# Scores of two key groups in one block-diagonal product; three steps of the second half put in another order

## The chip, the cores and the metric

The kernel runs on one NeuronCore of one Trainium2 chip. The metric is the device time of one execution in microseconds (us), and a kernel's time is the median of its runs.

## The reference

The kernel computes two transformer blocks on 512 tokens of width 1024, all in float32. The first block is a feed-forward layer, a mixing layer, a second feed-forward layer; the second block is a retention layer and a stick-breaking attention layer. The change touches only the attention of the mixing layer, which has three groups of four heads of width 64:

```
DILATED_GROUPS = ((128, 1), (512, 4), (2048, 16))      # window, dilation of each group
q, k, v = parts of (u @ w_in), each (1, 512, 12 heads, 64)
q, k = apply_partial_rope(q), apply_partial_rope(k)    # rotates the first 16 of 64 columns
for each group g:  s = q . k * 64 ** -0.5 over the keys that the window allows
                   m = max(s);  p = exp(s - m);  o = p @ v / sum(p)
alpha = softmax over the three groups of their log denominators;  o = sum(alpha * o)
```

## The kernel before

Every float32 product is made of three passes on TensorE (PE): an operand is split into a rounded high part (written by ScalarE, ACT) and the rest (written by VectorE, DVE: source minus high part), and `passes` multiplies high by high, high by low and low by high. Weights come in slabs through SyncE's queue into two slots `raw`; ACT writes `w_hi` (L668), DVE writes `w_lo` (L1377), and only then may PE use the slab (`w_ready`). All engines run their own program in order, joined by semaphores. The order of the work is written out by hand in each engine's block.

**Halves.** The mixing attention runs twice, a = 0 and a = 1, each for two of the four heads of every group. In a half, `qk` makes q and k of the three groups (g = 0, 1, 2; o = 0 for q, 1 for k): PE projects (512 columns, 24 passes), ACT copies the high part to `stage` (L689), DVE the low part (L1401), PE multiplies with a rotation matrix (`rotate`, L2614, L2615), DVE forms the two rope products (L1716, L1725) and their sum (L1728), and `rope_done` splits the result. In `rope_done` the three groups are treated unlike:

- g = 0: rows 0 to 63 of the tile are one head, rows 64 to 127 the other. ACT writes `q_both` or `k_both` in two instructions of 64 rows each (L908), and DVE writes `q_low` or `k_rest` in two of 64 rows (L1739). Then GpSimd's queue moves half tiles to the other 64 rows.
- g = 1, 2, k: one ACT instruction of 128 rows writes `k_hi[:, g - 1]` (L900) and one DVE instruction writes `k_lo[:, g - 1]` (L1731).
- g = 1, 2, q: ACT writes `q_pair[:, 0]` (L905), DVE writes `q_pair[:, 1]` in two instructions of 256 columns (L1734), and GpSimd's queue copies it (L618) into `q_head[j]`, which holds head j's 64 rows and zeros in the other 64.

After `qk` DVE and ACT do the pooling branch (half 0 alone: `pool_row`, L1827; `pool_window`, L1837 to L1842; `pool_low`) and the split of the values (`mix_values`: ACT L934, DVE L1453, reading two blocks of `values` at a time). DVE's program is one list: `rope_done` of the last k, the four pool rows, and among these the `w_lo` of the slabs that PE's `values` need.

**Units.** A half has 8 attention units (4 residues of the token number times 2 heads). `scores(a, k)` makes 768 scores a row: a mask over 512 keys of group 0 (L2675), a mask over 256 keys of groups 1 and 2 (L2676), group 0's product in two passes of 512 columns (L2677, L2678), and for each of groups 1 and 2 three passes of 128 columns (L2449, L2450, L2451 with `q_head`). DVE takes the row maximum (L1773), ACT the exponential (L941), PE turns it with six transposes (`turn`, L2692) into two banks of `acc`, ACT and DVE split it (L961 and L963, L1796 and L1798), PE multiplies with the values (L2717), and DVE adds the two parts (L1812), which gives the two banks back (`acc_free`). `attend` issues on PE, for each k: `scores(k + 3)`, `turn(k + 1)`, `values of k`, and for k of 4 and over some filling passes. `scores(a, k)` for k of 2 and over waits until the exponential of unit k - 2 is taken.

In half 1 PE runs the four blocks of the last `values` with the other steps between: the last rotation after block 0, `first_score(1)` after block 1, `scores(1, 1)` after block 2, then `attend`. DVE takes both maxima and then splits the last values; ACT likewise takes both exponentials and then the last values.

Of the kernel before, what the change touches and what calls it, by code (L numbers as in the profile page):

```python
# [17 lines left out]
F32 = mybir.dt.float32  # L18
# [5 lines left out]
P = 128  # L24
# [86 lines left out]
def block_kernel(nc, dram, out):  # L111
    with ExitStack() as ctx:
# [8 lines left out]
        with ExitStack() as under:  # L121
            q_both = [sb(f"q_both{j}", [P, TOK], F32R, under) for j in range(2)]
            k_both = [sb(f"k_both{j}", [P, TOK], F32R, under) for j in range(2)]
            k_rest = [sb(f"k_rest{j}", [P, TOK], F32R, under) for j in range(2)]
            q_pair = sb("q_pair", [P, 2, TOK], F32R, under)
# [116 lines left out]
        with ExitStack() as scope:  # L242
# [13 lines left out]
            with ExitStack() as inner:  # L256
                q_head = [sb(f"q_head{j}", [P, 2, N_GROUPS - 1, TOK], F32R, inner) for j in range(2)]
                k_hi = sb("k_hi", [P, N_GROUPS - 1, TOK], F32R, inner)
                k_lo = sb("k_lo", [P, N_GROUPS - 1, TOK], F32R, inner)
                va = sb("va", [P, TB, N_GROUPS * GROUP_HEADS, 2, HEAD], F32R, inner)  # L260
                stage = sb("stage", [P, 4 * KEYS], F32R, inner)
                fold = sb("fold", [P, 3 * HEAD], F32, inner)
                rope_a = sb("rope_a", [P, 2, TOK], F32, inner)
                band = sb("band", [P, 2 * DIL - 1, P], mybir.dt.bfloat16, inner)
                classes = sb("classes", [P, 2, P], mybir.dt.bfloat16, inner)
                ident_b = sb("ident_b", [P, P], mybir.dt.bfloat16, inner)
                neg_max = sb("neg_max", [P, UNITS], F32, inner)
                den = sb("den", [P, UNITS], F32, inner)
                rden = sb("rden", [P, UNITS], F32, inner)
                rcount = sb("rcount", [P, 2 * PAD], F32, inner)  # L270
                mix_b11 = sb("mix_b11", [P, TB, TOK // 2], F32, inner)
                mix_b12 = sb("mix_b12", [P, TB, TOK // 2], F32, inner)
                mix_b22 = sb("mix_b22", [P, TB, TOK // 2], F32, inner)
# [140 lines left out]
        pair_low_ready = sem("pair_low_ready")  # L414
        head_landed = sem("head_landed")
# [156 lines left out]
        def _(pool):  # L572
# [29 lines left out]
            for j, rows in enumerate(head_rows[::-1]):  # L602
                nc.gpsimd.memset(k_rest[j][rows, :].bitcast(F32), 0.0).then_inc(rest_clear, 1)
                nc.gpsimd.memset(q_head[j][rows, :, :, :].bitcast(F32), 0.0).then_inc(rest_clear, 1)

            def other_halves(a):
# [8 lines left out]
                for g in range(N_GROUPS - 1):  # L615
                    pool.wait_ge(pair_low_ready, (N_GROUPS - 1) * a + g + 1)
                    for j in range(2):
                        pool.dma_start(q_head[j][own[j], :, g, :], q_pair[own[j], :, :]).then_inc(head_landed, 16)  # L618
# [37 lines left out]
        def _(act):  # L656
            n, s, u, b = Count(), Count(), Count(), Count()
            val, turn, pairs = Count(), Count(), Count()
# [235 lines left out]
            def rope_done(g, o):  # L894
# [4 lines left out]
                if g and o:  # L899
                    ins = nc.scalar.activation(k_hi[:, g - 1, :], t(o), ACT.Copy, scale=QK_SCALE[o])  # L900
                elif g:
                    if pairs.k:
                        act.wait_ge(head_landed, 2 * 16 * pairs.k)
                    pairs.next()
                    ins = nc.scalar.activation(q_pair[:, 0, :], t(o), ACT.Copy, scale=QK_SCALE[o])  # L905
# [111 lines left out]
            exps(0)  # L1017
            exps(1)
            mix_values(2, 1)
# [347 lines left out]
        def _(dve):  # L1367
# [354 lines left out]
            def rope_done(g, o, split_after):  # L1722
# [7 lines left out]
                if g and o:  # L1730
                    stt(k_lo[:, g - 1, :], t(o), QK_SCALE[o], k_hi[:, g - 1, :].bitcast(F32), ALU.mult, ALU.subtract).then_inc(op_ready, 1)  # L1731
                elif g:
                    for j, cols in enumerate((EARLY, LATE)):
                        stt(q_pair[:, 1, cols], t(o)[:, cols], QK_SCALE[o], q_pair[:, 0, cols].bitcast(F32),  # L1734
                            ALU.mult, ALU.subtract).then_inc(pair_low_ready if j else op_ready, 1)
                    dve.wait_ge(pair_low_ready, lows.next())
# [159 lines left out]
            scores(0)  # L1896
            scores(1)
            mix_values(2, 1)
# [525 lines left out]
        def _(pe):  # L2424
# [242 lines left out]
            def scores(a, k):  # L2667
# [11 lines left out]
                for g in range(N_GROUPS - 1):  # L2679
                    last = passes(narrow[:, P * g:P * (g + 1)], [q_head[head][:, i, g, plain[r]] for i in range(2)],  # L2680
                                  (k_hi[:, g, plain[r]], k_lo[:, g, plain[r]]), False, g == N_GROUPS - 2)
# [58 lines left out]
            def first_score(a):  # L2740
                pe.wait_ge(op_ready, op.at())
                pe.wait_ge(rest_clear, 4)
                pe.wait_ge(both_landed, 4 * 16 * (a + 1))
                pe.wait_ge(head_landed, 2 * (N_GROUPS - 1) * 16 * (a + 1))
# [14 lines left out]
            def first_query(c):  # L2759
# [5 lines left out]
                if c == DC - 1:  # L2765
# [5 lines left out]
            values(x, plain, {(0, DC - 1): lambda: rotate_last(1), (1, DC - 1): lambda: first_score(1),  # L2771
                              (2, DC - 1): lambda: scores(1, 1)})
# [396 lines left out]
def lay_out(a):  # L3169

    w = {}
    for f, full in zip(("ffn1", "ffn2"), FULL):
# [11 lines left out]
    w["mix_qk"] = np.stack([np.stack([np.stack([cols[2 * g + c], cols[qc + 2 * g + c]], 1)  # L3184
                                      for g in range(N_GROUPS)]) for c in range(2)]).reshape(2, N_GROUPS, P, SLAB)
# [100 lines left out]
```

## Time and profile before

| | us |
|---|---|
| median of 3 runs | 1863.39 (1862.91 to 1864.31) |
| the profiled execution, its own time | 1862.57 |
| its span | 1860.8 |
| PE busy in the span | 1845.2 (99%) |
| PE weight loads busy | 1627.8 (87%) |
| DVE busy | 1324.6 (71%) |
| ACT busy | 879.1 (47%) |
| mean granted TensorE clock | 0.998 |

The span is the time from the first to the last instruction of the program; some 1.8 us of the execution lie around it. A matmul is shown with a duration that contains the latency of the array, so PE looks busy where one matmul's tail covers a short wait: what a pass costs is the distance from its start to the next start, and what a wait costs is what that distance has too much.

### The profile page before, as it was taken

How to read it: one execution, taken by the hardware profiler on the slowest of the kernel's cores; microseconds unless marked ns; L12 is line 12 of the kernel's file. 1: busy time of each engine (PE TensorE's matmuls, PEld its weight loads, DVE VectorE, ACT ScalarE, POOL GpSimd, SP SyncE). 2: the span in 40 equal slices, each digit the busy share in tenths (PEclk: the TensorE clock that was granted, in tenths of full speed). 3: DMA queues.
4: the chain of work that ended last, by engine and by line, in shares of the span. 5: the costliest groups of instructions: out<-in, count | busy, mean ns of one | idle time of the engine just before them, and what ended most of it. 6: DMA issues, size and time to landing. Idle time of an engine off the chain costs nothing.

```text
span 1860.8 us, 27165 instructions
## 1 busy us (share of the span) xinstructions
PE 1845.2 (99%) x10801; PEld 1627.8 (87%) x10807; DVE 1324.6 (71%) x1778; ACT 879.1 (47%) x1170; POOL 73.3 (4%) x96
## 2 busy tenths in 40 slices
PE   9999999999999999999999999999999999999997
PEld 7998998888889989989998888888888888888886
DVE  8875887888778888856888745463647776666666
ACT  6652664435355535634653332423336644444445
POOL 0000000120000000000000000000000000000000
PEclk9999999999999999999999999999999999999999
DMA  6744763462317526654753222122221222212213
GB/s 213 184 122 125 197 171 101 176 151 70 118 46 210 147 91 175 164 160 123 195 153 117 91 91 91 68 93 79 99 88 48 91 88 72 91 70 88 90 68 91
DMA packets 51506, 218.86 MB, mean 118 GB/s; under 512 B 5856, under 2 KB 8448, under 8 KB 39888
## 3 DMA queue, kind: packets, MB, share of 16 engines
q1 hardware_dynamic: 38960, 180.90, 28.9%
q0 software_dynamic: 12016, 36.04, 9.8%
q8 instruction: 69, 1.13, 0.2%
q10 hardware_dynamic: 432, 0.56, 0.1%
q14 instruction: 29, 0.24, 0.0%
HBM read 205.41 MB, written 5.77 MB: 113 GB/s over the span
## 4 chain that ended last, share of the span: by engine, by line
PE 73%; DVE 5%; ACT 2%; issue 1%; DMA 0%; DVEq 0%; POOL 0%; ACTq 0%
PE acc L2449 16%; PE acc L2451 16%; PE acc L2450 16%; PE acc L2456 4%; PE acc L2455 4%; PE acc L2457 4%; PE att L2450 2%; PE att L2451 2%; PE att L2449 2%; DVE w_lo L1377 1%; PE att L2455 1%; PE att L2457 1%; PE att L2456 1%; PE acc L2717 1%; PE acc L2692 1%
## 5 line engine op out<-in xcount | busy, mean ns | idle before, releaser
L1377 DVE TENSOR_TENSOR w_lo<-raw,w_hi 128x2048 fp32r<-128x2048 f32 (+1 forms) x120 | 271.0, 2258 | 69.8 <-ACT w_hi L668 68.9
L668 ACT ACTIVATE w_hi<-raw 128x2048 fp32r<-128x2048 f32 (+1 forms) x120 | 226.1, 1884 | 120.5 <-PE acc L2451 106.3
L2449 PE MATMUL acc<-x_hi,w_hi 128*128 128x512 f32 x712 | 280.9, 394 | 0.6 <-DVE x_lo L1440 0.3
L2451 PE MATMUL acc<-x_hi,w_lo 128*128 128x512 f32 x712 | 277.4, 390 | 0.0
L2450 PE MATMUL acc<-x_lo,w_hi 128*128 128x512 f32 x712 | 277.3, 389 | 0.0
L2449 PEld LDWEIGHTS acc<-x_hi,w_hi 128*128 128x128 f32 x712 | 133.7, 188 | 30.5 <-issue 2.9
L2450 PEld LDWEIGHTS acc<-x_lo,w_hi 128*128 128x128 f32 x712 | 133.7, 188 | 29.0 <-issue 1.6
L2451 PEld LDWEIGHTS acc<-x_hi,w_lo 128*128 128x128 f32 x712 | 133.7, 188 | 28.0
L2455 PE MATMUL acc<-xt_hi,w_hi 128*128 128x256 f32 x516 | 144.5, 280 | 0.0
L2457 PE MATMUL acc<-xt_hi,w_lo 128*128 128x256 f32 x516 | 144.3, 280 | 0.0
L2456 PE MATMUL acc<-xt_lo,w_hi 128*128 128x256 f32 x516 | 144.3, 280 | 0.0
L2450 PE MATMUL acc<-g_lo,w_hi 128*128 128x512 f32 x352 | 137.0, 389 | 0.0
L2449 PE MATMUL acc<-g_hi,w_hi 128*128 128x512 f32 x352 | 137.0, 389 | 0.0
L2451 PE MATMUL acc<-g_hi,w_lo 128*128 128x512 f32 x352 | 136.9, 389 | 0.0
L767 ACT ACTIVATE tmp<-acc 128x256 f32<-128x256 f32 x172 | 65.3, 380 | 80.2 <-PE acc L2457 72.8
L2455 PEld LDWEIGHTS acc<-xt_hi,w_hi 128*128 128x128 f32 x516 | 98.2, 190 | 0.0
L2456 PEld LDWEIGHTS acc<-xt_lo,w_hi 128*128 128x128 f32 x516 | 96.9, 188 | 0.0
L2457 PEld LDWEIGHTS acc<-xt_hi,w_lo 128*128 128x128 f32 x516 | 96.9, 188 | 0.0
L2455 PE MATMUL acc<-x_hi,wc_hi 128*128 128x256 f32 x344 | 95.0, 276 | 0.0
L2457 PE MATMUL acc<-x_hi,wc_lo 128*128 128x256 f32 x344 | 95.0, 276 | 0.0
L2456 PE MATMUL acc<-x_lo,wc_hi 128*128 128x256 f32 x344 | 94.9, 276 | 0.0
L2451 PEld LDWEIGHTS acc<-g_hi,w_lo 128*128 128x128 f32 x352 | 66.1, 188 | 13.7
(487 smaller groups left out, 4663.5 us busy)
## 6 DMA issues: line engine op xcount, KB each, us to landing
raw<-in_ret_head SPq DMA_DIRECT2D x24, 1024.0 KB, 4.8
raw<-in_ffn_down SPq DMA_DIRECT2D x32, 704.0 KB, 4.2
raw_c<-in_ffn_seven SPq DMA_DIRECT2D x37, 512.0 KB, 5.2
raw<-in_ffn_seven SPq DMA_DIRECT2D x33, 512.0 KB, 4.8
raw<-in_ffn_seven POOLq DMA_DIRECT2D x33, 512.0 KB, 7.6
raw<-in_ffn_seven SPq DMA_DIRECT2D x37, 256.0 KB, 4.6
raw<-in_ret_out SPq DMA_DIRECT2D x8, 1024.0 KB, 4.7
raw<-in_sb_v SPq DMA_DIRECT2D x8, 1024.0 KB, 4.7
```

The lines of the kernel that those rows point to most:

```text
L668: nc.scalar.activation(w_hi[:, slot, at:at + cols], raw[:, slot, 0:cols], ACT.Copy).then_inc(w_hi_ready, 1)
L767: nc.scalar.activation(dst, src, ACT.Copy).then_inc(snap_ready, 1)
L1377: tt(w_lo[:, slot, at:at + cols], raw[:, slot, 0:cols], w_hi[:, slot, at:at + cols].bitcast(F32), ALU.subtract).then_inc(w_ready, 1)
L2449: mm(dst, still[0], move[0], start=first, stop=False)
L2450: mm(dst, still[0], move[1], start=False, stop=False)
L2451: return mm(dst, still[1], move[0], start=False, stop=last)
L2455: mm(dst, still[0], move[0], start=first, stop=False, skip_group_check=True)
L2456: mm(dst, still[0], move[1], start=False, stop=False, skip_group_check=True)
L2457: return mm(dst, still[1], move[0], start=False, stop=last, skip_group_check=True)
L2692: last = nc.tensor.transpose(dst[i // TB][:, P * (i % TB):P * (i % TB) + P], tmp[:, at:at + P], ident[:])
L2717: last = mm(dst, va[:, k_blk, value_slot(g, head)].rearrange("p s d -> p (s d)"), turned_probs[:, k % 2, i].rearrange("p s q -> p (s q)"), ...
```

## The change

1. **Weights laid out by head.** In `mix_qk`, slabs 1 and 2 of a half no longer hold group 1 and group 2 with two heads each; slab 1 + j holds head j of both: rows 0 to 63 of a projected tile are group 1, rows 64 to 127 group 2.
2. **Block diagonals of k.** `k_hi` and `k_lo` become [128, 2 heads, 2, 512]: of head j, the first 512 columns have group 1's k in rows 0 to 63 and zeros below, the second 512 have zeros above and group 2's k in rows 64 to 127. ACT and DVE write them in two instructions of 64 rows each; the low part of the second counts on a new semaphore `half_low_ready`, and DVE waits for it before it goes on. GpSimd sets the zeros (four memsets of 64x1024 in the place of two of 64x2048).
3. **q without copies.** q of groups 1 and 2 is written straight to `q_hi` and `q_lo` by one instruction each; `q_pair`, `q_head`, their eight DMAs and ACT's wait for them go.
4. **Scores.** Three passes of 256 columns take the place of six of 128.
5. **Order of half 1.** `first_score(1)` comes after block 2 of the last values, `scores(1, 1)` after block 3; DVE and ACT split the last values between the first and the second maximum and exponential.

```diff
-                q_head = [sb(f"q_head{j}", [P, 2, N_GROUPS - 1, TOK], F32R, inner) for j in range(2)]
-                k_hi = sb("k_hi", [P, N_GROUPS - 1, TOK], F32R, inner)
-                k_lo = sb("k_lo", [P, N_GROUPS - 1, TOK], F32R, inner)
+                q_hi = sb("q_hi", [P, 2, TOK], F32R, inner)
+                q_lo = sb("q_lo", [P, 2, TOK], F32R, inner)
+                k_hi = sb("k_hi", [P, 2, 2, TOK], F32R, inner)
+                k_lo = sb("k_lo", [P, 2, 2, TOK], F32R, inner)
...
@@ GpSimd
-                nc.gpsimd.memset(q_head[j][rows, :, :, :].bitcast(F32), 0.0).then_inc(rest_clear, 1)
+                for part in (k_hi, k_lo):
+                    nc.gpsimd.memset(part[rows, :, j, :].bitcast(F32), 0.0).then_inc(rest_clear, 1)
...
-                for g in range(N_GROUPS - 1):
-                    pool.wait_ge(pair_low_ready, (N_GROUPS - 1) * a + g + 1)
-                    for j in range(2):
-                        pool.dma_start(q_head[j][own[j], :, g, :], q_pair[own[j], :, :]).then_inc(head_landed, 16)
@@ ACT, rope_done
                 if g and o:
-                    ins = nc.scalar.activation(k_hi[:, g - 1, :], t(o), ACT.Copy, scale=QK_SCALE[o])
+                    for i, rows in enumerate(head_rows):
+                        ins = nc.scalar.activation(k_hi[rows, g - 1, i, :], t(o)[rows, :], ACT.Copy, scale=QK_SCALE[o])
                 elif g:
-                    if pairs.k:
-                        act.wait_ge(head_landed, 2 * 16 * pairs.k)
-                    pairs.next()
-                    ins = nc.scalar.activation(q_pair[:, 0, :], t(o), ACT.Copy, scale=QK_SCALE[o])
+                    ins = nc.scalar.activation(q_hi[:, g - 1, :], t(o), ACT.Copy, scale=QK_SCALE[o])
@@ ACT, half 1
             exps(0)
+            mix_values(2, 1)
             exps(1)
-            mix_values(2, 1)
@@ DVE, rope_done
                 if g and o:
-                    stt(k_lo[:, g - 1, :], t(o), QK_SCALE[o], k_hi[:, g - 1, :].bitcast(F32), ALU.mult, ALU.subtract).then_inc(op_ready, 1)
+                    for i, rows in enumerate(head_rows):
+                        stt(k_lo[rows, g - 1, i, :], t(o)[rows, :], QK_SCALE[o], k_hi[rows, g - 1, i, :].bitcast(F32),
+                            ALU.mult, ALU.subtract).then_inc(half_low_ready if i else op_ready, 1)
+                    dve.wait_ge(half_low_ready, lows.next())
                 elif g:
-                    for j, cols in enumerate((EARLY, LATE)):
-                        stt(q_pair[:, 1, cols], t(o)[:, cols], QK_SCALE[o], q_pair[:, 0, cols].bitcast(F32),
-                            ALU.mult, ALU.subtract).then_inc(pair_low_ready if j else op_ready, 1)
-                    dve.wait_ge(pair_low_ready, lows.next())
+                    stt(q_lo[:, g - 1, :], t(o), QK_SCALE[o], q_hi[:, g - 1, :].bitcast(F32), ALU.mult, ALU.subtract).then_inc(op_ready, 1)
@@ DVE, half 1
             scores(0)
+            mix_values(2, 1)
             scores(1)
-            mix_values(2, 1)
@@ PE, scores
-                for g in range(N_GROUPS - 1):
-                    last = passes(narrow[:, P * g:P * (g + 1)], [q_head[head][:, i, g, plain[r]] for i in range(2)],
-                                  (k_hi[:, g, plain[r]], k_lo[:, g, plain[r]]), False, g == N_GROUPS - 2)
+                last = passes(narrow[:, 0:2 * P], (q_hi[:, head, plain[r]], q_lo[:, head, plain[r]]),
+                              (k_hi[:, head, :, plain[r]], k_lo[:, head, :, plain[r]]), False, True)
@@ PE, first_score
-                pe.wait_ge(rest_clear, 4)
+                pe.wait_ge(rest_clear, 6)
                 pe.wait_ge(both_landed, 4 * 16 * (a + 1))
-                pe.wait_ge(head_landed, 2 * (N_GROUPS - 1) * 16 * (a + 1))
+                pe.wait_ge(half_low_ready, (N_GROUPS - 1) * (a + 1))
@@ PE, half 1
-            values(x, plain, {(0, DC - 1): lambda: rotate_last(1), (1, DC - 1): lambda: first_score(1),
-                              (2, DC - 1): lambda: scores(1, 1)})
+            values(x, plain, {(0, DC - 1): lambda: rotate_last(1), (2, DC - 1): lambda: first_score(1),
+                              (3, DC - 1): lambda: scores(1, 1)})
@@ lay_out
+    def one_head(first, c, j):
+        return np.concatenate([cols[first + 2 * g + c][..., HEAD * j:HEAD * (j + 1)] for g in range(1, N_GROUPS)], -1)
+
+    w["mix_qk"] = np.stack([np.stack([np.stack([cols[c], cols[qc + c]], 1)]
+                                     + [np.stack([one_head(0, c, j), one_head(qc, c, j)], 1) for j in range(2)])
+                            for c in range(2)]).reshape(2, N_GROUPS, P, SLAB)
```

## Rows read from the trace of the kernel before

**Rows 1.** The page, busy time of each engine, us, share, instructions.
```profile
PE 1845.2 (99%) x10801; PEld 1627.8 (87%) x10807; DVE 1324.6 (71%) x1778; ACT 879.1 (47%) x1170; POOL 73.3 (4%) x96
```
**Rows 2.** Busy time of PE, PEld, DVE, ACT, POOL (instructions), clock, DMA, in one stretch.
```profile
386.00:428.00 42.00, 41.93 (x263) 37.23 (x263) 34.81 (x52) 16.10 (x19) 7.39 (x8) 1.00 0.60 146
```
**Rows 3.** Timeline of PE, start and duration in us: 256-column and 128-column passes, a turn.
```profile
498.73 0.28 PE L2451 MATMUL acc<-w_hi,x_lo 128*128 128x256 f32 x1
...
501.11 0.28 PE L2451 MATMUL acc<-w_hi,x_lo 128*128 128x256 f32 x1
...
511.33 0.22 PE L2449 MATMUL att<-k_hi,q_head 128*128 128x128 f32 x1
...
511.95 0.84 PE L2692 MATMUL acc<-ident,tmp 128*128 128x128 f32 x6
```
**Rows 4.** Timeline of PE, ACT and DVE through one attention unit, and the next turns.
```profile
519.78 0.85 PE L2692 MATMUL acc<-ident,tmp 128*128 128x128 f32 x6
...
520.44 0.60 ACT L961 ACTIVATE stage<-acc 128x512 fp32r<-128x512 f32 x1 [1.11 <-PE acc L2692]
...
521.14 0.69 DVE L1796 TENSOR_TENSOR stage<-acc,stage 128x512 fp32r<-128x512 f32 x1 [0.26 <-ACT stage L961]
...
522.08 0.41 DVE L1812 TENSOR_REDUCE o_even<-acc 128x128 f32<-128x256 f32 x1
...
522.64 0.84 PE L2692 MATMUL acc<-ident,tmp 128*128 128x128 f32 x6
...
528.37 0.30 PE L2692 MATMUL acc<-ident,tmp 128*128 128x128 f32 x1
```
**Rows 5.** Timeline of DVE, half 0: rope_done of k (g = 0), q and k (g = 1).
```profile
372.13 0.69 DVE L1728 TENSOR_TENSOR tmp<-tmp 128x512 f32<-128x512 f32 x1
374.16 1.41 DVE L1739 SCALAR_TENSOR_TENSOR k_rest<-tmp,k_both 64x512 fp32r<-64x512 f32 x2 [1.34 <-ACT k_both L908]
375.60 0.69 DVE L1401 TENSOR_TENSOR stage<-acc,stage 128x512 fp32r<-128x512 f32 x1
...
379.72 0.69 DVE L1728 TENSOR_TENSOR tmp<-tmp 128x512 f32<-128x512 f32 x1
...
381.90 0.69 DVE L1401 TENSOR_TENSOR stage<-acc,stage 128x512 fp32r<-128x512 f32 x1
...
383.83 0.69 DVE L1728 TENSOR_TENSOR tmp<-tmp 128x512 f32<-128x512 f32 x1
...
385.94 0.69 DVE L1401 TENSOR_TENSOR stage<-acc,stage 128x512 fp32r<-128x512 f32 x1
```
**Rows 6.** Timeline of DVE and PE weight loads, half 0, where its first values begin.
```profile
405.31 2.29 DVE L1377 TENSOR_TENSOR w_lo<-raw,w_hi 128x2048 fp32r<-128x2048 f32 x1
...
407.65 0.19 PEld L2449 LDWEIGHTS acc<-w_hi,x_hi 128*128 128x128 f32 x1 [0.43 <-DVE w_lo L1377]
```
**Rows 7.** Timeline of DVE and PE, entry of half 0 into its units.
```profile
437.42 0.88 DVE L1453 SCALAR_TENSOR_TENSOR va<-acc,r_tok,va 128x256 fp32r<-128x256 f32 x2 [1.86 <-ACT va L934]
...
442.80 0.85 PE L2692 MATMUL acc<-ident,tmp 128*128 128x128 f32 x6 [0.18 <-DVE o_even L1812]
```
**Rows 8.** Timeline of PE, DVE and ACT, entry of half 1 into its units.
```profile
497.92 0.51 PE L2614 MATMUL att<-stage,rot_r 128*128 128x512 f32 x1 [0.53 <-DVE stage L1401]
...
500.81 0.69 DVE L1731 SCALAR_TENSOR_TENSOR k_lo<-tmp,k_hi 128x512 fp32r<-128x512 f32 x1 [0.70 <-ACT k_hi L900]
...
502.17 0.27 PE L2676 MATMUL att<-classes,ident_b 128*128 128x256 bf16 x1 [0.79 <-DMA q_head<-q_pair]
...
508.18 1.81 DVE L1773 TENSOR_REDUCE neg_max<-att 128x1 f32<-128x768 f32 x2
509.15 0.90 ACT L941 ACTIVATE tmp<-att,neg_max 128x768 f32<-128x768 f32 x1 [6.27 <-DVE neg_max L1773]
...
511.80 0.88 DVE L1453 SCALAR_TENSOR_TENSOR va<-acc,r_tok,va 128x256 fp32r<-128x256 f32 x2 [1.81 <-ACT va L934]
...
512.63 0.38 PE L2675 MATMUL att<-band,ident_b 128*128 128x512 bf16 x1
```

More of the change, by code:

```diff
@@ L124, in block_kernel @@
             k_rest = [sb(f"k_rest{j}", [P, TOK], F32R, under) for j in range(2)]
-            q_pair = sb("q_pair", [P, 2, TOK], F32R, under)
         h = sb("h", [P, DC, TOK])
@@ L413, in block_kernel @@
         both_landed = sem("both_landed")
-        pair_low_ready = sem("pair_low_ready")
-        head_landed = sem("head_landed")
+        half_low_ready = sem("half_low_ready")
         park_landed = sem("park_landed")
@@ L657, in _ @@
             n, s, u, b = Count(), Count(), Count(), Count()
-            val, turn, pairs = Count(), Count(), Count()
+            val, turn = Count(), Count()
             def prep(cols=SLAB, seg=0):
@@ L3183, in lay_out @@
     qc = heads // P
-    w["mix_qk"] = np.stack([np.stack([np.stack([cols[2 * g + c], cols[qc + 2 * g + c]], 1)
-                                      for g in range(N_GROUPS)]) for c in range(2)]).reshape(2, N_GROUPS, P, SLAB)
+    def one_head(first, c, j):
[3 more added lines that the diff above has]
+                            for c in range(2)]).reshape(2, N_GROUPS, P, SLAB)
     v_cols = columns(w_in, 2 * heads, heads).reshape(P, DC, N_GROUPS, 2, 2 * HEAD)
```

## The prediction

> **What bounds the kernel now.** I read the page's busy times first: PE is busy 99% of the span [rows 1], so a saving on PE seems to be worth its full length. That figure hides short waits, so I then read starts. In the stretch where half 0 goes from rope to pooling PE shows 41.93 of 42 us busy, but DVE has 34.81 [rows 2], and what remains to DVE is waits for ACT within its own chain. The first matmul of that half's first values starts only when DVE has finished `w_lo`: 405.31 + 2.29 = 407.60, start at 407.65 [rows 6]. So there DVE sets PE's time, with no slack.
>
> The timeline of the units gives the second bound. Turns on PE start at 519.78 and 522.64, 2.86 apart with a unit's scores between; the two steps from there to 528.37, one with scores and one with filling passes in their place, take 5.73 = 2 x 2.865 [rows 4]. The same period for unlike work says that the loop is not PE's own. It closes as: turn at 519.78, ACT splits at 520.44 (+0.66), DVE at 521.14 (+0.70), DVE's reduction at 522.08 (+0.94) ends at 522.49 (+0.41) and gives the banks back, and the next turn starts 0.15 later at 522.64. 0.66 + 0.70 + 0.94 + 0.41 + 0.15 = 2.86. The turn at 442.80 in half 0 even shows its wait for that reduction [rows 7]. PE is a co-bound: free of waits a turn starts about 0.1 after the last pass of the scores, so its own loop would be some 0.05 shorter at best. It is not longer than the chain.
>
> **The change part by part.** All against the profiled execution, 1862.57.
>
> *Scores.* Six passes of 128 columns took from 511.33 to 511.95 = 0.62. A 256-column pass costs (501.11 - 498.73) / 21 = 0.113 [rows 3], three of them 0.34. Saved on PE: 0.28 a unit, 16 units, 4.5 us. The loads of the q tiles are halved with them. The strided second level of the new moving tile is not in the trace; its bounds are 0 (as the two-level tiles of the values) and the whole saving, if each row of 128 went at the old price. I take 0.
>
> How much of it reaches the end? In a half, units 3 to 7 are scored inside the 2.86 loop. What PE saves there it waits: 0. In half 0, units 0 to 2 are scored before the loop. But DVE comes to its split of the values at 437.42 after waiting for ACT [rows 7], ACT was at the exponential of unit 1, that waited for the maximum of unit 1, and this stood behind DVE's pooling; from 437.42 DVE's list runs without a gap to the first split of the turned unit. That chain contains no pass of scores. So half 0 gives 0 of its 2.2 us, bound 0 to 0.3 (a little where PE waits in the pooling). Half 1 is worked out below.
>
> *q.* One instruction in the place of two of 256 columns and a wait. With two, sum to next step is 379.72 to 381.90 = 2.18; with one instruction of 512 columns, as k now, 383.83 to 385.94 = 2.11 [rows 5]. -0.07 for each q that lies on DVE's chain. The eight copies leave GpSimd's queue; what stood behind them there (copies for `mix_b`) comes some 6 us earlier and is needed a hundred us later in half 1. 0.
>
> *k.* This is the price. Two ACT and two DVE instructions of 64 rows take the place of one and one of 128 rows. Group 0 already does so, and its rows show that 64 rows cost as long as 128: DVE's two take 1.41 together, against 0.69 for one of 128, and it waits 1.34 for ACT where the wait for one is 0.70. From the sum to the next step: 372.13 to 375.60 = 3.47 for the split k, 2.11 for the whole one [rows 5]. +1.36 us for each k of groups 1 and 2, four of them, all on DVE's chain. Bounds: 0.6, if the second halves would run beside other work, to 1.5.
>
> *Half 0.* Behind the first such k stand on DVE: the low part of the next projection, its rope, and through ACT's order the next `w_hi`; behind the second one the four pool rows and the `w_lo` of rows 6. I find no idle time there that isn't a wait for ACT that itself waited for DVE. So 1.36 + 1.36 - 0.07 = 2.65 goes to the `w_lo` that PE waits for at 407.65, and from there PE, DVE and ACT shift together. Half 0: +2.65 (bounds +1.0 to +3.0).
>
> *Half 1.* Times in the frame of before. The first k and the two q move DVE by 1.36 - 2 x 0.07, and by 0.11 more because the step after this k didn't wait for its end and now does: +1.33. The low part that the last rotation waits for comes that much later, so PE's rotation at 497.92 [rows 8] goes to 499.25. Block 1 begins 0.58 after it (its third pass was at 498.73, less two of 0.113), and blocks 1 and 2 with 24 passes each end at 499.83 + 2 x 2.72 = 505.3. The low part of the second k ended at 500.81 + 0.69 = 501.5 and ends 1.33 + 1.36 later, at 504.2, so `first_score` in its new place doesn't wait, and the wait for the q copies (0.79 shown) is gone. Up to here PE is only some 1 us late and saves 0.28 twice more. But DVE: the next `w_lo` waits for `w_hi`, and this for ACT's second half of k: 1.33 + 0.64 (1.34 - 0.70 of rows 5) + 0.1, since the two halves don't overlap in ACT as whole ones did, is 2.1 later than before; the sums for `mix_b` follow and the first maximum starts at 508.18 + 2.1 = 510.28.
> Now the new order. Exponential 0 starts 0.97 after the maximum (508.18 to 509.15), at 511.25; ACT then splits the last values from 512.15 (0.90); DVE follows 0.87 later, at 513.02 (before, 511.80 stood about that far behind ACT's start, two exponentials after 509.15), takes 0.79, and only then the maximum of unit 1: 513.81. Its exponential runs 514.80 to 515.79. `scores(1, 3)` on PE waits for exactly this one; it starts at 515.86, before at 512.63 [rows 8]: 3.23 later, less the 0.28 saved in it, and the turn of unit 1 and with it the loop of 2.86 come 2.95 later. Before, the exponential of unit 1 followed that of unit 0 at once (0.90 behind 509.15), was over by 511, and nobody waited for it. So half 1 costs +2.9, of which 2.1 come from k and 0.8 from the order; the seven savings of scores in it do nothing. Bounds: -0.6, if PE's list set the entry (next part), to +3.5.
>
> *Memsets.* The same bytes in four pieces; they are over some 50 us before they are needed. 0.
>
> Sum: 2.65 + 2.9 = +5.55; 1862.57 + 5.55 = 1868.1. The median shown is 0.82 above the profiled execution, so I say 1868.9.
>
> **The rivals.**
> (1) *PE is the bound after all.* For it: 99% busy, and the waits that go, 0.79 at the first score. Then the 4.5 of the passes and 0.8 of the wait come through and DVE's added time lies beside PE: 1863.39 - 5.3 = 1858.1. Against it: the period of 2.86 with and without scores, and rows 6. I give it 0.10. Here the trace can be weighed against the Trainium skill ("TensorE: Matmul & The Clock Gate", Back-to-back issue gap): by it an isolated pass costs the columns / 2.4 plus 2.5 ns, so 56 ns for 128 columns, and six narrow passes would cost no more than three wide ones; this rival would then give back only the 0.8 of the wait, 1862.6. Rows 3 disagree: 0.62 / 6 = 0.10 us for a narrow pass, nearly that of a wide one. Whoever leaves this out loses nothing of the sum.
> (2) *PE's list sets the entry of half 1.* Half 0 costs 2.65, but DVE and ACT in half 1 have enough room; then half 1 has the rotation +1.33, the wait -0.95 (0.79 shown, with what the tail covers), and three scores -0.84: -0.5. 1863.39 + 2.15 = 1865.5. For it: DVE sat idle 1.81 before 511.80, room in which a delay could vanish. Against it: that room is a wait for ACT behind exponential 1, and the new order puts one more such wait in. 0.20.
> (3) *The split runs beside itself*, so that each k costs about 0.7: half 0 +1.3, half 1 +2.2, 1866.9. Against it: the 1.41 and 1.34 of rows 5. 0.08.
> The forecast: 0.62.
>
> **How the numbers follow.** Faster or slower by over 0.2% (3.7 us) is about what a measurement of this kernel tells from no change. Forecast, 1868.9 +-1.5, lies at +5.5; nearly all of it is slower. (2) and (3) are within 0.2%, with some of each beyond. (1) is faster. Faster 0.11, same 0.27, slower 0.62. The range leaves out (1) and takes in (2): 1863.5 to 1870.7.
>
> **What would show it.** In the profile after: the k splits of 64 rows on DVE twice 0.69; the first matmul of half 0's values still waiting for `w_lo`, 2.6 later (at 410.2 to 410.4); turns in the units still 2.86 apart, now with a wait of about 0.3 for the reduction in front of each; in half 1 a wait of PE for an exponential of several us in front of the third and fourth scores. I would be wrong if the period fell to about 2.6, if the first values of half 0 began before 409, or if the fourth scores of half 1 found their exponential taken.

## The result and the profile after

The kernel after takes 1868.88 us (median of 11 runs, 1867.58 to 1870.71), the kernel before, beside it, 1862.90 (11 runs, 1862.43 to 1864.31): ratio 1.0031, 95% interval 1.0023 to 1.0039. It is 6.0 us slower; 1868.9 had been forecast, which is 5.5 above the 1863.39 of before that the forecast started from. The profiled execution of after took 1869.26 us, its span is 1867.4.

The page's busy times answer to [rows 1]. PE is busy 2.7 us less and the kernel is 6 us longer:

```profile
PE 1842.5 (99%) x10753; PEld 1623.2 (87%) x10759; DVE 1327.2 (71%) x1778; ACT 881.4 (47%) x1174; POOL 68.6 (4%) x90
```

The stretch of [rows 2], same columns. PE had 41.93 busy there and has 39.36:

```profile
386.00:428.00 42.00, 39.36 (x242) 34.74 (x242) 34.94 (x52) 14.44 (x17) 5.99 (x6) 1.00 0.53 132
```

Those 2.57 us are one wait. The first line is DVE's and the second PE's timeline at the first values of half 0, as in [rows 6]:

```profile
408.28 2.28 DVE L1371 TENSOR_TENSOR w_lo<-raw,w_hi 128x2048 fp32r<-128x2048 f32 x1
...
410.62 0.39 PE L2443 MATMUL acc<-w_hi,x_hi 128*128 128x256 f32 x1 [2.57 <-DVE w_lo L1371]
```

Why DVE's list came later is in its timeline of one k, which answers to the last part of [rows 5]. From the sum to the next step it takes 387.62 - 384.15 = 3.47 (2.11 before):

```profile
384.15 0.69 DVE L1722 TENSOR_TENSOR tmp<-tmp 128x512 f32<-128x512 f32 x1
386.19 1.40 DVE L1726 SCALAR_TENSOR_TENSOR k_lo<-tmp,k_hi 64x512 fp32r<-64x512 f32 x2 [1.34 <-ACT k_hi L897]
387.62 0.69 DVE L1395 TENSOR_TENSOR stage<-acc,stage 128x512 fp32r<-128x512 f32 x1
```

The entry of half 1, PE, DVE and ACT together, answers to [rows 8]:

```profile
502.25 0.50 PE L2608 MATMUL att<-stage,rot_r 128*128 128x512 f32 x1 [1.94 <-DVE stage L1395]
...
513.34 0.95 DVE L1767 TENSOR_REDUCE neg_max<-att 128x1 f32<-128x768 f32 x1
514.33 0.90 ACT L935 ACTIVATE tmp<-att,neg_max 128x768 f32<-128x768 f32 x1 [6.35 <-DVE neg_max L1767]
...
515.37 0.39 PE L2669 MATMUL att<-band,ident_b 128*128 128x512 bf16 x1 [1.69 <-ACT tmp L935]
...
516.08 0.88 DVE L1447 SCALAR_TENSOR_TENSOR va<-acc,r_tok,va 128x256 fp32r<-128x256 f32 x2 [1.79 <-ACT va L928]
...
516.87 1.81 DVE L1767 TENSOR_REDUCE neg_max<-att 128x1 f32<-128x768 f32 x2
517.85 0.90 ACT L935 ACTIVATE tmp<-att,neg_max 128x768 f32<-128x768 f32 x1 [1.81 <-DVE neg_max L1767]
...
519.13 0.27 PE L2670 MATMUL att<-classes,ident_b 128*128 128x256 bf16 x1 [1.79 <-ACT tmp L935]
```

PE waits for each of the first two exponentials (515.37, 519.13), and the second stands behind the last values: split (516.08), maximum (516.87), exponential (517.85). The loop answers to [rows 4]; PE's turns stay 2.86 apart, the last of them again with a wait shown for DVE's reduction:

```profile
522.46 0.28 PE L2445 MATMUL att<-k_hi,q_lo 128*128 128x256 f32 x1
522.89 0.85 PE L2685 MATMUL acc<-ident,tmp 128*128 128x128 f32 x6
...
525.75 0.85 PE L2685 MATMUL acc<-ident,tmp 128*128 128x128 f32 x6
...
531.48 0.73 PE L2685 MATMUL acc<-ident,tmp 128*128 128x128 f32 x5 [0.15 <-DVE o_odd L1806]
```

By starts, the turn comes 522.89 - 522.46 = 0.43 behind the last pass of the scores. A pass costs 0.12, so PE waits about 0.31 there. In before the last pass of the scores stands in front of the turn at 522.64 [rows 4] like this:

```profile
522.48 0.27 PE L2451 MATMUL att<-k_hi,q_head 128*128 128x128 f32 x1
```

That is 0.16, with 0.11 for a pass, so a wait of 0.05. What the scores save has turned into a wait.

To compare kernels I measure starts from the first rotation of half 0 (360.71 in before, 361.11 in after; what PE runs ahead of it is the same). The turn of the last unit starts at 96.41 in before and 98.95 in after for half 0, and at 170.52 and 176.10 for half 1: +2.54, and 3.04 more. What follows differs by under 0.7.

### The profile page after: what moved, and what is told of

The parts are those of the page before. It is cut to its first block, busy times and chain, and to the rows that moved or that the text cites. A ratio compares the mean times of both kernels' runs of the same rounds, so it can differ in the third digit from the quotient of the medians.

```text
span 1867.4 us, 27066 instructions
## 1 busy us (share of the span) xinstructions
PE 1842.5 (99%) x10753; PEld 1623.2 (87%) x10759; DVE 1327.2 (71%) x1778; ACT 881.4 (47%) x1174; POOL 68.6 (4%) x90
## 3 DMA queue, kind: packets, MB, share of 16 engines
q8 instruction: 68, 1.11, 0.2%
## 4 chain that ended last, share of the span: by engine, by line
PE 71%; DVE 6%; ACT 2%; issue 1%; DVEq 0%; ACTq 0%
PE acc L2443 16%; PE acc L2445 16%; PE acc L2444 16%; PE acc L2449 4%; PE acc L2450 4%; PE acc L2451 4%; PE att L2444 2%; PE att L2445 2%; PE att L2443 2%; DVE w_lo L1371 1%; PE att L2449 1%; PE att L2451 1%; PE att L2450 1%; DVE tmp L1722 0%; DVE tmp L1719 0%
## 5 line engine op out<-in xcount | busy, mean ns | idle before, releaser
L2443 PE MATMUL acc<-w_hi,x_hi 128*128 128x512 f32 (+1 forms) x224 | 77.0, 344 | 2.6 <-DVE w_lo L1371 2.6
```

Of the source, the lines that this page charges most:

```text
L2443: mm(dst, still[0], move[0], start=first, stop=False)
```

## The experiments

Each kernel was timed beside the kernel before. Its medians in the three groups of runs were 1862.85, 1862.97 and 1862.92. A start that stands in no line below, like 49.65, is measured from the first rotation of half 0.

**The order alone.** After with half 1's order as it was in before:

```
-  exps(0); mix_values(2, 1); exps(1)                      # ACT
+  exps(0); exps(1); mix_values(2, 1)
-  scores(0); mix_values(2, 1); scores(1)                  # DVE
+  scores(0); scores(1); mix_values(2, 1)
-  (2, DC - 1): first_score(1), (3, DC - 1): scores(1, 1)  # PE
+  (1, DC - 1): first_score(1), (2, DC - 1): scores(1, 1)
```

> The changed kernel with its block diagonals, but PE, DVE and ACT of half 1 in the order of before: first scores after block 1 of the last values, second after block 2, last values split behind both maxima. Theory (the exponential of unit 1 sets the entry of half 1, and the new order puts a split of the values in front of it): PE waits about 1.8 us for the low part of k in front of the first scores, but the exponential of unit 1 then runs right behind that of unit 0, the wait in front of the fourth scores (1.9 us in the changed kernel) is gone, and the turns of units 2 and on come 0.8 us earlier: 1868.0 against 1868.9. Rival (the new order is needed to hide the late k): the 1.8 us wait of PE is carried to the end, 1870 or more.

1867.65 us, ratio 1.0025 (1.0016 to 1.0035): 1.2 less than after. PE's timeline, the first scores and the turn of unit 2:

```profile
507.38 0.38 PE L2669 MATMUL att<-band,ident_b 128*128 128x512 bf16 x1 [1.63 <-DVE k_lo L1726]
...
521.85 0.85 PE L2685 MATMUL acc<-ident,tmp 128*128 128x128 f32 x6
```

The first scores now wait 1.63 for `k_lo`, but both exponentials follow one another and the fourth scores find theirs taken; the turn of unit 2 comes 0.96 earlier (521.85 - 361.03 against 522.89 - 361.11). The new order costs about 1 us, as worked out (0.8), and not more. The other 5 are not its doing.

**The split alone.** Before, with k of groups 1 and 2 split in two instructions of 64 rows on ACT and on DVE, into the same tiles. DVE and PE's first scores wait for the second half, as in after:

```
-  nc.scalar.activation(k_hi[:, g - 1, :], t(o), ...)
+  for rows in head_rows:
+      nc.scalar.activation(k_hi[rows, g - 1, :], t(o)[rows, :], ...)      # and k_lo alike
```

> The kernel before with one thing of the change: ACT and DVE write k_hi and k_lo of groups 1 and 2 in two instructions of 64 rows each, into the same tiles; q, its copies, scores and order as before. Theory (the split k lies on the DVE chain that PE waits for): the first matmul of half 0's first values comes 2.7 us later (407.65 to 410.3), half 1 enters its units 2.1 us later, sum +4.8: 1867.7 against 1862.9. Rival (PE is the bound and DVE's work lies beside it): 1862.9.

1869.00 us, ratio 1.0032 (1.0022 to 1.0043). No pass of PE is changed and the whole loss is there: rival (1) is out. It is 1.3 above what was expected. The first values come at 49.65 (46.94 in before): +2.71, as expected. But the last turn of half 0 comes 3.86 late, and half 1 adds 2.53 where 2.1 had been expected. What half 0 has too much in this execution is in the clock. These are windows around that wait; the seventh figure of a row, behind the length and the five engines, is the granted clock as a share of 2.4 GHz. Under them stands PE's timeline:

```profile
408.00:412.00 4.00, 1.66 (x8) 1.66 (x9) 3.89 (x5) 2.93 (x2) 1.93 (x2) 0.72 1.19 176
412.00:416.00 4.00, 4.00 (x32) 4.00 (x32) 3.70 (x7) 0.07 (x1) 0.00 (x0) 0.85 1.16 186
```

```profile
410.34 0.58 PE L2454 MATMUL acc<-w_hi,x_hi 128*128 128x256 f32 x1 [2.73 <-DVE w_lo L1379]
410.72 0.41 PE L2455 MATMUL acc<-w_lo,x_hi 128*128 128x256 f32 x1
...
413.06 0.34 PE L2454 MATMUL acc<-w_hi,x_hi 128*128 128x256 f32 x1
413.24 0.28 PE L2455 MATMUL acc<-w_lo,x_hi 128*128 128x256 f32 x1
...
413.70 0.28 PE L2456 MATMUL acc<-w_hi,x_lo 128*128 128x256 f32 x1
```

From 410.72 to 413.06 a pass takes 2.34 / 11 = 0.213, then (413.70 - 413.24) / 4 = 0.115. So after its wait PE ran at its lower level of 1.2 GHz; twelve passes cost 12 x 0.098 = 1.2 us. The profile of after shows a clock of 1.00 behind the same wait. How many of the eight runs had such a fall is not on record; three list a mean clock of 0.997, the others 0.998, so the median's 1.3 is not fully explained.

**Six narrow passes.** After, with 3 x 128 columns for each of groups 1 and 2 in place of 3 x 256:

```
-  last = passes(narrow[:, 0:2 * P], (q_hi[:, head, plain[r]], q_lo[:, head, plain[r]]),
-                (k_hi[:, head, :, plain[r]], k_lo[:, head, :, plain[r]]), False, True)
+  for g in range(N_GROUPS - 1):
+      last = passes(narrow[:, P * g:P * (g + 1)], (q_hi[:, head, plain[r]], q_lo[:, head, plain[r]]),
+                    (k_hi[:, head, g, plain[r]], k_lo[:, head, g, plain[r]]), False, g == N_GROUPS - 2)
```

> The changed kernel with the scores of groups 1 and 2 in six passes of 128 columns instead of three of 256, from the same block diagonals. Theory (what scores save on PE is waited away): 0.28 us a unit come back on PE, 4.5 us in all, but the turns stay 2.86 us apart, with the wait in front of them gone, and the total moves by +0.3 us (one pass group behind the awaited exponential in half 1), at most +0.6: 1869.2. Rival (PE is the bound): +4.5, 1873.4.

1869.08 us, ratio 1.0034 (1.0021 to 1.0047), after 1868.88: no difference that six runs can show. PE's timeline in half 1:

```profile
522.72 0.85 PE L2686 MATMUL acc<-ident,tmp 128*128 128x128 f32 x6
...
525.59 0.84 PE L2686 MATMUL acc<-ident,tmp 128*128 128x128 f32 x6
```

The turns stay 2.87 apart, and the last one comes 0.28 later than in after, as expected of one group of passes behind an awaited exponential. The wide passes, the point of the new layout, are worth next to nothing in this kernel, and not 4.5 us.

**The reduction first.** After, with DVE's reduction of a finished unit ahead of the low parts of the next:

```
-  if k + 1 < UNITS: low_probs(k + 1)
   dve.wait_ge(mixed, mix.next())
   nc.vector.tensor_reduce(o_unit[k % 2][:, k // 2, :], ...).then_inc(acc_free, 2)
+  if k + 1 < UNITS: low_probs(k + 1)
```

> The changed kernel with one step of DVE in the units moved: the reduction that gives back the two banks (L1806) now stands before the split of the next turned unit (L1790, L1792), not behind it. Theory (the loop of 2.86 us is turn, ACT split, DVE split, DVE reduction, next turn): the reduction leaves the loop, and where DVE has no weights to split (half 1, up to the fifth turn) the period falls to PE's own 2.53 to 2.6 us, about 0.3 less for 4 steps; in half 0 DVE's work of some 2.8 us a unit takes over, -0.1 us a unit. Sum -1.3 us: 1867.6. Rival (the period has another cause, PE or the exponentials): no change, 1868.9.

1867.77 us, ratio 1.0029 (1.0019 to 1.0038). The timeline of this kernel's PE in half 1:

```profile
525.19 0.82 PE L2685 MATMUL acc<-ident,tmp 128*128 128x128 f32 x6
...
527.72 0.82 PE L2685 MATMUL acc<-ident,tmp 128*128 128x128 f32 x6
```

The turns are 2.53 apart: the chain over DVE's reduction was what held the loop at 2.86. From the second turn to the last half 1 takes 15.61, 1.5 less than after (17.15). The whole kernel gains 1.1, near the 1.3 expected. The low parts of the last unit now come late and take something back: its values wait 0.82 in each half (a line of this wait stands below, in the kernel with all edits). This profiled execution also had two falls of the clock (0.81 in 408 to 412, 0.58 in 502 to 506); what the median has of them is not shown.

**The low part earlier.** After, with one step of DVE's list moved:

```
-  pool_window(i)
   if i == 1: prep()          # w_lo of the first values
+  pool_window(i)
```

> The kernel after, with one step of VectorE's list moved: in the first half the low part of the weights of the first values (w_lo, 2.28 us, it started at 408.28 and ended PE's wait of 2.57 us at 410.62) is formed before the pooling window of the second row instead of behind it. Theory: what lies between the end of the split of k and the loop is VectorE's whole list, so the first values start about 2.4 us earlier, but the later instructions of the list (pooled rows, maxima, low part of the turned probabilities) come no earlier, and the turn of unit 2 of half 0 stays at 84.6 us behind the first rotation: total 1868.9 (1867.5 to 1869.5). If it is the wait of PE at that place which costs the time: 1866.5. If only the fall of the granted clock behind that wait costs something now and then, the median is about 1868 and the spread of the runs is narrower.

1869.76 us, ratio 1.0039 (1.0025 to 1.0052), against 1868.9 expected: no gain, as the theory has it. It is 0.9 above after, which five runs do not set clear of noise (1868.40 to 1870.58, after 1867.58 to 1870.71), but the trace shows a loss that the theory had not. The first values come 2.7 earlier (46.82), and PE waits 13 us later. First DVE's, then PE's timeline:

```profile
411.51 1.12 DVE L1395 TENSOR_TENSOR pool_lo<-tmp,pool_hi 128x512 fp32r<-128x512 f32 x1 [1.19 <-ACT pool_hi L681]
```

```profile
423.71 0.39 PE L2443 MATMUL acc<-w_hi,x_hi 128*128 128x256 f32 x1 [3.43 <-DVE w_lo L1371]
```

In after the `w_lo` filled the time in which DVE waits for `pool_hi` of row 1; moved, it leaves 1.19 idle there, and DVE's next steps come 1.07 later. Behind the wait of 3.43 the clock fell too (seventh figure):

```profile
424.00:428.00 4.00, 4.00 (x24) 4.00 (x23) 3.79 (x9) 0.38 (x1) 0.00 (x0) 0.60 0.75 260
```

The slow passes of the values make DVE wait 2.17 for ACT's part of them, in after 1.40; that is the other 0.77 of the 1.83 by which the turn of unit 2 comes later. Four of the five runs list a mean clock of 0.997 or less and take 1869.6 to 1870.6; the fifth lists 0.998 and takes 1868.40. So the edit's own loss may be smaller than the medians say. What counts is DVE's whole list with its idle times, and not where in it PE's wait shows. The next edits follow from that.

**Fill the gap.** After, with a `w_lo` formed while ACT writes the `k_hi` of the last group (half 0: the one that stood in front; half 1: the one that stood behind, for which ACT also writes its `w_hi` before its part of `rope_done`):

```
   tt(t(o), t(o), t(2 + o), ALU.add)          # the sum, in rope_done
+  prep()                                     # w_lo
   dve.wait_ge(hi_ready, hi.next())
```

> The kernel after, with VectorE's forming of a low part of weights (2.28 us in half 0, 1.76 us in half 1) put into the 1.34 us in which VectorE waits for ScalarE's two half instructions k_hi of the last key group, in both halves; ScalarE's high part of the same slab comes before its part of the split in half 1. Theory (the split costs because VectorE's list is the bound and stands idle 1.34 us beside it): half 0 gains 1.3 (the idle time) and up to 2.3 at the first values, half 1 gains 1.3: total 1866.3 (1865 to 1867.5). Rival, that the split's own 0.7 us of VectorE per instruction and the chain k_hi, k_lo, DMA of the second half of k set the time: nothing gained or 1 us lost, 1869 to 1870, since k_lo comes 0.9 us later.

1864.54 us, ratio 1.0011 (1.0002 to 1.0020): 4.3 less than after, more than expected (2.6). DVE's timeline in half 0, sum, `w_lo`, `k_lo`, without idle time:

```profile
392.18 0.69 DVE L1722 TENSOR_TENSOR tmp<-tmp 128x512 f32<-128x512 f32 x1
392.79 2.28 DVE L1371 TENSOR_TENSOR w_lo<-raw,w_hi 128x2048 fp32r<-128x2048 f32 x1
394.99 1.40 DVE L1728 SCALAR_TENSOR_TENSOR k_lo<-tmp,k_hi 64x512 fp32r<-64x512 f32 x2
```

The turn of unit 2 of half 0 goes from 84.62 to 82.22: 2.4 = the 1.34 at `k_hi`, and 1.11 that this `w_lo` itself had waited for `w_hi` in its old place. The latter I had not counted. The last turn comes 3.98 earlier.

**The same on before.** Before with that edit:

> The kernel before, with the edit of f1_fill_the_gap alone (low part of the weights formed in the time in which VectorE waits for k_hi). Theory: in before PE is the bound at the entry of half 0 (its turn of unit 2 in g came only 0.2 us earlier), and half 1 gains the 0.7 us of the gap at most: 1862.4 (1861.8 to 1863.2). So what f1 gave back, 4.3 us, was the cost of the split; with the gap filled in both, the split still costs f1 - g1 = about 2 us. Rival, that f1's edit is worth as much without the split: 1858.6.

1863.07 us, ratio 1.0001 (0.9992 to 1.0010). It gains nothing, so what it gave after was the price of the split. The 0.7 expected in half 1 doesn't come either: the `w_lo` takes 1.75 in a gap of 0.70, `k_lo` comes that much later, and PE's first scores wait for it:

```profile
502.93 0.27 PE L2676 MATMUL att<-classes,ident_b 128*128 128x256 bf16 x1 [1.18 <-DVE k_lo L1733]
```

With the gap filled in both, the change costs 1864.54 - 1863.07 = 1.5.

**Halves that overlap.** After, with a semaphore for the first of ACT's two halves, so that DVE's first half runs beside ACT's second:

```
+  if i == 0: ins.then_inc(half_high_ready, 1)                 # ACT, behind each k_hi
-  dve.wait_ge(hi_ready, hi.next())                            # DVE
+  if g and o: dve.wait_ge(half_high_ready, highs.next())
+  else: dve.wait_ge(hi_ready, hi.next())
   ...
   for i, rows in enumerate(head_rows):
+      if i: dve.wait_ge(hi_ready, hi.next())
       stt(k_lo[rows, g - 1, i, :], ...)
```

> The kernel after, with a semaphore of its own for the first of ScalarE's two half instructions k_hi, so that VectorE forms the first half of k_lo while ScalarE forms the second half of k_hi: VectorE's idle time at a split of k goes from 1.34 to 0.67 us. Theory (VectorE's list is the bound, three of the four splits of k lie in it): 0.67 less at each, 2.0 us in all, 1866.8 (1866 to 1867.8). Rival, that only the number of instructions costs and the wait is hidden: 1868.9.

1866.69 us, ratio 1.0021 (1.0012 to 1.0030): 2.2 less than after, 2.1 forecast. DVE's timeline, idle time 0.70 in place of 1.34:

```profile
385.16 1.40 DVE L1734 SCALAR_TENSOR_TENSOR k_lo<-tmp,k_hi 64x512 fp32r<-64x512 f32 x2 [0.70 <-ACT k_hi L898]
```

Three splits at 0.64 are 1.9, the last turn comes 1.85 earlier: 1.26 in half 0, 0.59 in half 1.

**All together, with the change and without it.** On top of the filled gap: the three sums of `mix_b` (3.7 us of DVE) go from the entry of half 1 into the second `qk`, the reduction goes first, and PE and ACT enter half 1 in another order (DVE's stays that of after, and is put so in the kernel without the change too):

```
   elif last and g == 0: gather(0)                                      # DVE, in qk
+      <the three sums of mix_b>
-  {(0, ..): rotate_last(1), (2, ..): first_score(1), (3, ..): scores(1, 1)}
+  {(1, ..): rotate_last(1), (3, ..): (first_score(1), scores(1, 1))}
-  mix_values(2, 0); exps(0); mix_values(2, 1); exps(1)                  # ACT
+  mix_values(2, 0); mix_values(2, 1); exps(0); exps(1)
```

> f1 and three more edits on the kernel after: the three sums of mix_b (3.7 us of VectorE) go from the entry of half 1 to the first step of the second pass over q and k; PE runs the last rotation behind the second block of values and the first two scores behind the fourth; VectorE reduces a finished unit ahead of the next unit's low parts (the edit of e4_reduce_first), and ScalarE and VectorE take the last values ahead of the first exponentials. Theory (VectorE's list bounds the entries of both halves and its place in the loop costs 0.3 us a unit): half 0 -2.3 - 1.3, half 1 -1.5 - 3.7 (of which the second pass over q and k gives back up to 3.7, its idle time there is 0.2 to 1.3 us a step) - 1.5: 1859.5 (1858 to 1863). Rival, that PE's list bounds the entry of half 1: 1864 to 1866, since the first scores come two blocks of values later.

> The same edits as f2_all_together on the kernel before (q as the block diagonal, six passes of 128 columns, k split in one instruction a part). Theory: before has 0.7 us less of VectorE at the two splits of k and 0.11 us more of PE per score; with VectorE's list relieved the wide passes are worth at most 4.5 us less 1.4: this kernel at 1860.7 (1859 to 1863), 1 us above f2. Rival, that the split stays the bound: this kernel 3 to 5 us below f2.

With the change 1860.10 us (1859.46 to 1861.09), ratio 0.9986 (0.9977 to 0.9995); without it 1863.17, ratio 1.0001 (0.9992 to 1.0010). The four edits that take 8.8 us from after take nothing from before, and beside them the change is worth 3.1 us, three times what I expected. PE's timeline of half 1 without the change, and with it:

```profile
516.51 0.84 PE L2692 MATMUL acc<-ident,tmp 128*128 128x128 f32 x6
...
519.33 0.84 PE L2692 MATMUL acc<-ident,tmp 128*128 128x128 f32 x6
```

```profile
515.16 0.82 PE L2685 MATMUL acc<-ident,tmp 128*128 128x128 f32 x6
...
517.68 0.82 PE L2685 MATMUL acc<-ident,tmp 128*128 128x128 f32 x6
...
531.99 0.98 PE L2710 MATMUL acc<-stage,va 128*128 128x256 f32 x6 [0.82 <-DVE stage L1799]
```

With the chain over DVE gone from both, a unit takes 2.82 with narrow passes and 2.52 with wide ones: now PE's own work is the period, and the 0.28 a unit of the forecast's first step is there. It is there in full in three steps of half 1. From the turn of unit 2 to that of unit 7 half 0 is 0.33 shorter with wide passes and half 1 0.91. So the periods are 1.2 of the 2.5 by which the last turn comes earlier, and the rest lies in the entries of the halves, which no run divides further. The last line is the price of the reduction first: the values of the last unit wait 0.82.

**The last unit as before.** The kernel with all edits, but in the last step of each half the low parts come first again:

```
+  if k == UNITS - 2: low_probs(k + 1)
   dve.wait_ge(mixed, mix.next())
   <the reduction>
-  if k + 1 < UNITS: low_probs(k + 1)
+  if k + 1 < UNITS - 1: low_probs(k + 1)
```

> f2_all_together, but in the last step of each half VectorE takes the last unit's low parts ahead of the reduction, as in the kernel before and after: in f2 PE waited 0.9 and 0.8 us for them there. Expected: 2 x 0.8 less than f2: 1858.5 (1857.5 to 1859.5). Rival, that ScalarE's exponentials or the banks set that end: 1860.1.

1858.32 us (1857.96 to 1858.99), ratio 0.9977 (0.9967 to 0.9986): the fastest kernel here, 4.6 below before and 10.6 below after. The values of the last unit follow the filling passes without a wait.

**Without the order.** That kernel with after's order at the entry of half 1:

> f3 with the order of half 1's entry as in the kernel after (rotation behind block 0 of the values, first scores behind block 2, second behind block 3, exponentials between the last values): only the gap filled, the three sums of mix_b moved and the reduction first. Theory: moving the sums frees 3.7 us of VectorE before the entry, so its waits (1.9 us of the rotation for the low part of stage, 1.6 us of the fourth scores) shrink to under 1 us in all; the order is then worth 0.5 to 1: 1859.3 (1858.3 to 1860.5). Rival, that the order was the main part of f2: 1861.5 or more.

1860.96 us, ratio 0.9991 (0.9981 to 1.0000): 1.7 above the expectation's 1859.3, 2.6 above the last kernel. PE's timeline at the last rotation, and the windows around it, clock in the seventh figure:

```profile
498.60 0.79 PE L2610 MATMUL att<-stage,rot_r 128*128 128x512 f32 x1 [1.95 <-DVE stage L1395]
...
499.61 0.41 PE L2445 MATMUL acc<-w_hi,x_hi 128*128 128x256 f32 x1
...
501.96 0.32 PE L2447 MATMUL acc<-w_hi,x_lo 128*128 128x256 f32 x1
```

```profile
496.00:500.00 4.00, 2.05 (x10) 1.65 (x9) 2.56 (x5) 2.49 (x3) 0.00 (x0) 0.83 0.01 2
500.00:504.00 4.00, 4.00 (x29) 4.00 (x28) 3.93 (x5) 1.53 (x3) 0.00 (x0) 0.75 0.09 16
```

I was wrong that moving the sums would shorten the rotation's wait: it is 1.95, in after 1.94. The sums stand behind the low part for which it waits; what they free is later. And behind the wait the clock fell: passes (501.96 - 499.61) / 11 = 0.214 apart. Of this kernel's 11 runs seven took 1859.9 to 1861.2 and four 1862.5 to 1863.2; the profiled one, 1862.66, is of the four. These four list a mean clock of 0.997, six of the seven others 0.998 or 0.999, so the slower ones probably had such a fall and the others not.

## Why the prediction was right

Its time was right (1868.9, measured 1868.88), and so were nearly all of its steps. That it fits to 0.02 is luck: the forecast added 5.5 to a before of 1863.39, and what was measured is 6.0 above a before of 1862.90, so two errors of 0.5 cancel. By the turn of the last unit the traces are 5.58 apart, forecast 5.55. Starts in after are compared with the forecast's plus the 0.40 by which the first rotation starts later in this trace.

- *k, +1.36 each.* 3.47 against 2.11, as taken. On its own, in before, it gave as much as the whole change, with a fall of the clock in the profiled execution. Halving DVE's idle part gave 2.2 back, filling it 4.3. The lower bound of 0.6, the split beside other work, is what the overlapped halves reach, not what the change does.
- *Half 0, +2.65 at `w_lo`.* 2.57 in PE's busy time, 2.54 at the last turn. The forecast took off 0.07 for one q; the chain has two, and 2 x 1.36 - 2 x 0.07 = 2.58.
- *Half 1.* Rotation forecast at 497.92 + 2.65 + 1.33 + 0.40 = 502.30, measured 502.25. First exponential 514.30, measured 514.33; last values 516.07, measured 516.08; second maximum 516.86, measured 516.87; fourth scores 518.9, measured 519.13 at their second mask (the first is missing in the trace). In all 3.04, forecast 2.9. The two waits for exponentials, 1.69 and 1.79, are shorter than the "several us" named as a sign.
- *The order, 0.8 of it.* Undoing it gave 1.2, 0.96 of it at the turn of unit 2.
- *Scores, 0 of 4.5.* Six narrow passes in after: 0.28 at the last turn and no clear difference in time. The wait forecast in front of each turn, about 0.3, is there by starts (0.31), though the profile names it at few turns and with 0.15. The reason given, a loop of 2.86 that is DVE's chain and not PE's, held: the reduction moved, the same loop takes 2.53. So did the estimate that PE's own loop in before would be 0.05 shorter (2.82).
- *Rivals.* (1) is out by the split alone. (2) is out by the two waits of 1.69 and 1.79 for exponentials, which PE's list doesn't hide. (3) is out for the change, and true of the overlapped halves: 1866.69, its price 1866.9. What the forecast worked out from the Trainium skill's formula for an isolated pass ("TensorE: Matmul & The Clock Gate", Back-to-back issue gap), that six narrow passes cost PE no more than three wide ones, is out as well: with PE as the bound the narrow ones cost 2.82 - 2.52 = 0.30 us a unit. The same section says that its formula counts too little for small passes in a stream with a weight load for each, and has 81 ns for 128 columns there; the trace has 0.10 us [rows 3].

What the forecast did not have: the fall of the clock behind a long wait. In the split alone it cost 1.2 us of the profiled execution; in after it isn't in the profile. A fall of that size takes some 1.2 / 1867 = 0.0007 off a run's mean clock. The two slowest of the 11 runs of after (1870.71 and 1869.57) list 0.996 and 0.997, the others 0.998 or 0.999, so it may have struck these two; the median run lists 0.998, like the profiled one, in which it isn't. The runs of after spread over 3.1 us, the fastest kernel's over 1.0.

## What to carry to other kernels

Before work is taken from a 99% busy engine, ask whose chain sets the period where that work stands: here PE's 4.5 us were worth nothing as long as DVE's list set the time. With the gap filled, three sums and one reduction moved and the entry of half 1 reordered, the change was worth 3.1 net of its price, where these four edits without it gained nothing. A split into half tiles costs the consumer the full length of each half and the wait for both; put work that is due anyway into that wait, or hand over each half by itself. And read a list with its idle times: moving a late item forward helps only if it lands in a gap and leaves none.

## What the hardware showed

**A wait can halve the clock behind it.** After waits of 2.73 and 1.95 us PE ran at 1.2 GHz (passes of 256 columns 0.213 apart, not 0.115) for about 3 us, for 1.2 us of loss in the passes; in the profile of after waits of 2.57 and 1.94 at the same places left it at 1.00. Between 360 and 560 us the profiles of all kernels show 14 waits of PE of 1.9 us or more, and the granted clock fell behind five of them: these two, 2.58 and 1.94 with the reduction first, and 3.43 with the low part earlier. By the Trainium skill ("TensorE: Matmul & The Clock Gate", Part 1) the same kernel may show a different number of slow matmuls at its start from run to run. No run here tests its start; at the rotation two kernels' profiles agree with it in kind, as equal waits (1.94 and 1.95) had unlike clocks behind them.

**64 rows cost what 128 do.** Two DVE instructions of 64 x 512 took 1.40, one of 128 x 512 0.69. The Trainium skill's "VectorE: DVE Perf Modes" (Why `tensor_reduce` can't reduce along partition axis) has each partition as a lane of its own that streams along the free dimension; the rows agree.
